# A two-block transformer kernel on one core: other order of the first loads and splits, a norm weight spread by matmul, a last norm by token block, and two adjacent norms computed side by side

## What is computed

```
def rms_norm / rmsnorm(x, g):
    y = x * rsqrt(mean(x * x, axis=-1) + EPS)
    return y * g

def first_block(...):
    for l in range(2):
        x = x + 0.5 * swiglu(rms_norm(x, ffn1_norm[l]), ...)
        ...
        x = x + 0.5 * swiglu(rms_norm(x, ffn2_norm[l]), ...)
    return rms_norm(x, final_norm)

def second_block(...):
    for l in range(2):
        x = x + swiglu_half(rmsnorm(x, g_ffn1[l]), ...)
        ...
        x = x + swiglu_half(rmsnorm(x, g_ffn2[l]), ...)
    return rmsnorm(x, g_final)
```

## Time and profile before

| | us |
|---|---|
| median of 3 runs | 2466.97 (2466.48 to 2468.95) |
| the profiled execution's own time | 2469.05 |
| its span in the profile | 2467.3 |
| PE busy in the span | 2427.1 (98%) |
| DVE busy | 1391.4 (56%) |
| ACT busy | 1175.5 (48%) |
| HBM read | 426.12 MB, 173 GB/s over the span |

### The profile page before, as it was taken

The page is one execution under the profiler, slowest core; times in us unless marked ns, Lnnn a source line. Parts: engine busy times, 40 slices in busy tenths (PEclk is TensorE's granted clock), DMA queues, the critical chain, the costliest instruction groups (busy, mean ns, idle before and its releaser), DMA issues.

```text
span 2467.3 us, 31131 instructions
## 1 busy us (share of the span) xinstructions
PE 2427.1 (98%) x12132; PEld 2038.8 (83%) x12132; DVE 1391.4 (56%) x1297; ACT 1175.5 (48%) x1193; POOL 13.9 (1%) x12
## 2 busy tenths in 40 slices
PE   7999999999999999999999999999999999999998
PEld 6888988788888898888887888878888888887887
DVE  5457855554555577455546546447546456457554
ACT  5445654444444475444445444654445444554443
POOL 0000010000000001000000000000000000000000
PEclk9999999999999999999999999999999999999999
DMA  8554434365565553345555555545655555644653
GB/s 286 187 187 151 157 103 165 109 204 187 178 204 182 170 175 123 121 144 171 184 190 189 187 192 190 159 159 175 196 188 180 191 188 191 189 154 145 205 181 108
DMA packets 329059, 428.41 MB, mean 174 GB/s; under 512 B 15568, under 2 KB 294352, under 8 KB 328720
## 3 DMA queue, kind: packets, MB, share of 16 engines
q1 hardware_dynamic: 325104, 412.48, 51.6%
q10 hardware_dynamic: 3872, 14.75, 1.7%
HBM read 426.12 MB, written 1.05 MB: 173 GB/s over the span
## 4 chain that ended last, share of the span: by engine, by line
PE 93%; ACT 3%; DVE 2%; issue 1%; DMA 1%; ACTq 0%; DVEq 0%; SPq 0%
PE ps L829 28%; PE ps L831 28%; PE ps L830 28%; PE ps L971 2%; PE ps L842 2%; PE ps L1038 1%; ACT whi L451 1%; PE ps L1191 1%; ACT arena L465 1%; PE ps L1091 1%; PE ps L1174 1%; DVE wlo L1342 0%; PE ps L1228 0%; DMA xres<-in_x 0%; PE ps L1093 0%
## 5 line engine op out<-in xcount | busy, mean ns | idle before, releaser
L1342 DVE TENSOR_TENSOR wlo<-raw,whi 128x2048 fp32r<-128x2048 f32 (+1 forms) x395 | 895.5, 2269 | 534.6 <-ACT whi L451 534.4
L451 ACT ACTIVATE whi<-raw 128x2048 fp32r<-128x2048 f32 (+1 forms) x395 | 749.0, 1896 | 442.6 <-PE ps L831 430.4
L829 PE MATMUL ps<-whi,hT_hi 128*128 128x512 f32 x2240 | 890.4, 397 | 7.3 <-DVE hT_lo L1386 2.9
L831 PE MATMUL ps<-whi,hT_lo 128*128 128x512 f32 x2240 | 874.0, 390 | 0.0
L830 PE MATMUL ps<-wlo,hT_hi 128*128 128x512 f32 x2240 | 872.4, 389 | 0.0
L829 PEld LDWEIGHTS ps<-whi,hT_hi 128*128 128x128 f32 x2240 | 424.2, 189 | 92.9 <-issue 4.5
L831 PEld LDWEIGHTS ps<-whi,hT_lo 128*128 128x128 f32 x2240 | 424.0, 189 | 89.2
L830 PEld LDWEIGHTS ps<-wlo,hT_hi 128*128 128x128 f32 x2240 | 424.7, 190 | 82.2 <-issue 0.5
L829 PE MATMUL ps<-whi,aT_hi 128*128 128x512 f32 x640 | 249.9, 390 | 0.0
L831 PE MATMUL ps<-whi,aT_lo 128*128 128x512 f32 x640 | 249.2, 389 | 0.0
L830 PE MATMUL ps<-wlo,aT_hi 128*128 128x512 f32 x640 | 249.1, 389 | 0.0
(11 more groups left out here) (230 smaller groups left out, 1528.3 us busy)
## 6 DMA issues: line engine op xcount, KB each, us to landing
raw<-in_w_ffn SPq DMA_DIRECT2D x264, 512.0 KB, 4.2
raw<-in_w_in SPq DMA_DIRECT2D x144, 512.0 KB, 4.8
raw<-in_ffn_w_down SPq DMA_DIRECT2D x88, 512.0 KB, 4.1
raw<-in_ffn_w_up SPq DMA_DIRECT2D x87, 512.0 KB, 4.0
raw<-in_ffn_w_gate SPq DMA_DIRECT2D x87, 512.0 KB, 4.9
raw<-in_w_out SPq DMA_DIRECT2D x32, 512.0 KB, 4.1
gain<-in_gains ACTq DMA_DIRECT2D x17, 512.0 KB, 4.6
raw<-in_cross_wk SPq DMA_DIRECT2D x16, 512.0 KB, 4.2
```

The costliest lines, as they stand in the source:

```text
L451: act.activation(whi[:, s, :, 0:cols], raw[:, s, :, 0:cols], ACT.Copy).then_inc(hi_ready, 1)
L829: pe.matmul(out, l_hi, r_hi, start=first, stop=False, skip_group_check=True)
L831: return pe.matmul(out, l_lo, r_hi, start=False, stop=last, skip_group_check=True)
L1342: dve.tensor_tensor(wlo[:, s, :, 0:cols], raw[:, s, :, 0:cols], whi[:, s, :, 0:cols].bitcast(F32), ALU.subtract).then_inc(lo_ready, 1)
```

## The change

At the start, only one row of the first gain is loaded (1 x 1024). DVE writes 128 ones into one row of `prod`, and two matmuls of PE multiply the ones by the gain row, which leaves the gain on all partitions in PSUM banks 1 and 3. `first_piece` reads it from there. DVE does pieces 0 and 1, then the first splits, then pieces 2 and 3. ACT rounds unit 2 after the transposes of pieces 2 and 3 instead of before them. The five small loads leave SP's list, and together with table_a and `memx` they are issued by ACT behind the rounding of unit 4.

Between the blocks, `gain_final` puts `xres * final_gain` into a place of its own (`x_gained`) ahead of the split of unit 2, the second norm's sums are taken from `x_gained` without the first norm's factor, and that factor enters as the scale of the second Sqrt.

At the end, the last down unit goes through its pieces as 0, 2, 1, 3. The Sqrt table is loaded by a small activation ahead of the sums. Token block 0 gets its sum and root as soon as its two halves are there, and the second root takes its first half's sum as its bias. ACT issues the last of the four output DMAs.

```diff
@@ sync: ffn, and the output
                 gate_up(off, 0, 0)
-                if b == l == e == 0:
-                    for dst, src in ((lbt[:, :, :], lb), (onorm[:, :, :], out_norm.unsqueeze(0).broadcast_to([P, DEPTH, H_D])),
-                                     (fbias[:, :], f_bias), (wpool[:, :, :, :], w_pool), (pscale[:, :, :], pool_scale)):
-                        sp.dma_start(dst, src).then_inc(loaded, 16)
...
-            for i in range(PIECES):
-                sp.wait_ge(x_ready, PIECES * add_no(1, DEPTH, 0) + i + 1)
+            for n, i in enumerate(LAST_ORDER[:3]):
+                sp.wait_ge(last_out, n + 1)
                 sp.dma_start(piece(o, i), piece(xres, i)).then_inc(stored, 16)
@@ scalar
-            act.dma_start(gain[:, :], gains[0:1, :].broadcast_to([P, DM])).then_inc(gain_loaded, 16)
+            act.dma_start(gain[0:1, :], gains[0:1, :]).then_inc(gain_loaded, 16)
...
+            def joint_squares(n, add):
+                for t in range(TB):
+                    act.wait_ge(x_ready, PIECES * add + 2 + t + 1)
+                    act.activation(sq_junk[:, t * DM:(t + 1) * DM], x_gained[:, t, :], ACT.Square, accum_out=stat[:, 1, 0, t:t + 1]).then_inc(sq_sum, 1)
+                act.wait_ge(sq_sum, 2 * n + 2)
+                act.wait_ge(inv_ready, n)
+                for t in range(TB):
+                    root = act.activation(stat[:, 1, 1, t:t + 1], stat[:, 1, 0, t:t + 1], ACT.Sqrt, scale=stat[:, 1, 2, t:t + 1], bias=EPS)
+                root.then_inc(sq_done, 1)
+
+            def last_norm():
+                act.activation(fin[:, 6:8], ident[:, 0:2], ACT.Sqrt)
+                seen = PIECES * add_no(1, DEPTH, -1)
+                act.wait_ge(x_ready, seen + 2)
+                act.activation(sq_junk[:, 0:DM], xres[:, 0, :], ACT.Square, accum_out=fin[:, 0:1]).then_inc(last_sum, 1)
+                act.wait_ge(last_sum, 1)
+                act.activation(fin[:, 1:2], fin[:, 0:1], ACT.Sqrt, scale=1.0 / DM, bias=EPS).then_inc(last_root, 1)
+                for h in range(2):
+                    act.wait_ge(x_ready, seen + 3 + h)
+                    act.activation(sq_junk[:, DM + 512 * h:DM + 512 * (h + 1)], xres[:, 1, 512 * h:512 * (h + 1)], ACT.Square,
+                                   accum_out=fin[:, 2 + h:3 + h]).then_inc(last_sum, 1)
+                act.wait_ge(last_sum, 3)
+                act.wait_ge(last_bias, 1)
+                act.activation(fin[:, 5:6], fin[:, 3:4], ACT.Sqrt, scale=1.0 / DM, bias=fin[:, 4:5]).then_inc(last_root, 1)
+                act.wait_ge(last_out, PIECES)
+                i = LAST_ORDER[3]
+                act.dma_start(piece(out[0].rearrange("(t p) d -> p t d", p=P), i), piece(xres, i)).then_inc(stored, 16)
...
                     first_split_hi(1)
                     split_hi(b, l, 1)
-                split_hi(b, l, off + 2)
-                turn_out(T, (2, 3))
+                    turn_out(T, (2, 3))
+                    split_hi(b, l, off + 2)
+                else:
+                    split_hi(b, l, off + 2)
+                    turn_out(T, (2, 3))
...
                 if (b, l, e) == (1, 0, 0):
-                    act.wait_ge(inv_ready, n)
-                    squares(xres, n, add + 1, which=1, scale=[stat[:, 0, 2, t:t + 1] for t in range(TB)])
+                    joint_squares(n, add + 1)
@@ tensor
+            pe.wait_ge(first_ones, 1)
+            pe.wait_ge(gain_loaded, 16)
+            for n, bank in enumerate(GAIN_BANKS):
+                pe.matmul(ps[:, bank, :], ones_row, gain[0:1, n * 512:(n + 1) * 512], start=True, stop=True).then_inc(first_gain, 1)
             pe.wait_ge(ident_loaded, 16)
@@ vector
+            def gain_final():
+                for i in range(PIECES):
+                    dve.tensor_tensor(piece(x_gained, i), piece(xres, i), final_gain[:, i // 2 * 512:(i // 2 + 1) * 512], ALU.mult).then_inc(x_ready, 1)
+
             def final_scale(n):
-                inverse(n - 1)
-                for i in range(PIECES):
-                    dve.tensor_tensor(piece(xres, i), piece(xres, i), final_gain[:, i // 2 * 512:(i // 2 + 1) * 512], ALU.mult).then_inc(x_ready, 1)
+                dve.wait_ge(sq_done, n)
+                step(dve.reciprocal(stat[:, 0, 2, :], stat[:, 0, 1, :]))
+                dve.scalar_tensor_tensor(out=stat[:, 1, 2, :], in0=stat[:, 0, 2, :], scalar=1.0 / DM, in1=stat[:, 0, 2, :],
+                                         op0=ALU.mult, op1=ALU.mult).then_inc(inv_ready, 1)
+                for t in range(TB):
+                    scaled = dve.tensor_scalar(xres[:, t, :], x_gained[:, t, :], stat[:, 0, 2, t:t + 1], None, ALU.mult)
+                step(scaled)
                 dve.wait_ge(sq_done, n + 1)
-                for t in range(TB):
-                    last = dve.tensor_scalar(xres[:, t, :], xres[:, t, :], stat[:, 0, 2, t:t + 1], None, ALU.mult)
-                step(last)
...
                 if b == l == e == 0:
                     turn_out(T, (0, 1))
                     first_split_lo(1)
+                    first_piece(2)
+                    first_piece(3)
                     split_lo(b, l, 1)
                 turn_out(T, (2, 3))
+                if (b, l, e) == (1, 0, 0):
+                    gain_final()
                 split_lo(b, l, off + 2)
...
+            def last_output(off):
...
+                def scale(t, root):
+                    dve.wait_ge(last_root, t + 1)
+                    step(dve.reciprocal(fin[:, 8 + t:9 + t], fin[:, root:root + 1]))
+                    for h in range(2):
+                        dve.tensor_scalar(piece(xres, 2 * h + t), piece(xn, 2 * h + t), fin[:, 8 + t:9 + t], None, ALU.mult).then_inc(last_out, 1)
...
+                    if n == PIECES - 1:
+                        dve.wait_ge(last_sum, 2)
+                        dve.tensor_scalar(fin[:, 4:5], fin[:, 2:3], 1.0 / DM, EPS, ALU.mult, ALU.add).then_inc(last_bias, 1)
...
+            dve.memset(ones_row, 1.0).then_inc(first_ones, 1)
+            def first_piece(i):
+                dve.wait_ge(first_gain, i // 2 + 1)
+                dve.wait_ge(x_loaded[i], 16)
+                dve.sem_inc(x_ready, 1)
+                dve.tensor_tensor(piece(xn, i), piece(xres, i), ps[:, GAIN_BANKS[i // 2], :], ALU.mult).then_inc(xn_ready, 1)
+            first_piece(0)
+            first_piece(1)
```

More of the change, by code:

```diff
@@ L37 @@
 S_A, S_B = 3, 2
-V_A, V_B = 30, (12, 10)
+V_A, V_B = 30, (13, 12)
 A_FFN1 = 0
@@ L184, in build @@
         final_gain, joint_gain = zf, hq
+        x_gained = arena[:, 2048 + 6 * 1024:2048 + 8 * 1024].rearrange("p (t d) -> p t d", t=TB)
+        fin = sst[:, 0, :]
+        ones_row = prod[0:1, 0, 0:P]
+        GAIN_BANKS = (1, 3)
+        LAST_ORDER = (0, 2, 1, 3)
         fcs_f, fcs_c, fcs_t = (fcs[0:8, a:a + 256] for a in (0, 256, 768))
@@ L220, in build @@
         first_hi, first_lo = sem("first_hi"), sem("first_lo")
+        first_ones, first_gain = sem("first_ones"), sem("first_gain")
+        last_sum, last_bias, last_root, last_out = (sem(f"last_{n}") for n in ("sum", "bias", "root", "out"))
         tables_loaded = sem("tables_loaded")
@@ L524, in ffn @@
                 split_hi(b, l, off + 4)
+                if b == l == e == 0:
+                    for dst, src in ((lbt[:, :, :], lb), (onorm[:, :, :], out_norm.unsqueeze(0).broadcast_to([P, DEPTH, H_D])),
+                                     (fbias[:, :], f_bias), (wpool[:, :, :, :], w_pool), (pscale[:, :, :], pool_scale)):
+                        act.dma_start(dst, src).then_inc(loaded, 16)
+                    act.dma_start(cst[:, :], table_a).then_inc(tables_loaded, 16)
+                    act.dma_start(memx[:, :, :], mem[0].rearrange("(t p) d -> p t d", p=P)).then_inc(tables_loaded, 16)
                 with act.Fori(0, FF_STEPS - 2) as c:
@@ L818, in _ @@
                 assert count[0] == S_B, ("S_B", count[0])
-            squares(xres, norm_no(1, DEPTH, 0), add_no(1, DEPTH, -1))
+            last_norm()
         @block.tensor
@@ L904, in features_unit, with tall_unit @@
                     then[3]()
-            def tall_unit(b, l, off, lhs, bank, first, last, c=0, T=None, k0=0, signal=None, then={}):
+            def tall_unit(b, l, off, lhs, bank, first, last, c=0, T=None, k0=0, signal=None, then={}, order=range(PIECES)):
                 s = off % RING
                 wait_weights(b, l, off, c)
-                for i in range(PIECES):
-                    half, t = divmod(i, 2)
+                for i, at in enumerate(order):
+                    half, t = divmod(at, 2)
                     if T is not None and half == 0:
@@ L977, in down @@
                     tall_unit(b, l, off, lhs, ACC, first, last, c, signal=acc_done if last else None,
-                              then=then or (turn_ahead(b, T_next) if last else {}))
+                              then=then or (turn_ahead(b, T_next) if last else {}),
+                              order=LAST_ORDER if last and T_next is None else range(PIECES))
```

(3 more changed lines are left out.)

40 lines of the change are left out of this document (25 added, 15 removed).

## The result

The changed kernel takes 2459.04 us in the median of 6 executions (2458.09 to 2460.97), the kernel before 2467.69 of 7: ratio 0.9967, 95% interval 0.9957 to 0.9977. A seventh execution of the changed kernel, at a granted clock of 0.883 instead of 0.995, took 2594.6 and is left out of the median. The profiled execution took 2460.50 (span 2458.6), 8.55 less than the profiled one of before. The forecast was 2457.5, range 2453.5 to 2462.5.

A forecast was written before the change was run, and what follows sets the result against it. PE was taken to bound the kernel (93% of the span). Start -3.0, join -2.25 and -2.5, end -1.7 sum to -9.45 from 2469.05, 2459.6; the median 2.1 lower gives 2457.5 us, range 2453.5 to 2462.5.

The forecast's parts named there:

- Start, -3.0 forecast: At the start: PE's first product 3.5 us earlier, less a 0.5 stall from the swap; bounds -1.5 and -4.
- 512 KB are worth 2.3 us there: Start, ACT's queue: the smaller gain load makes x 2.3 us earlier, and the identity lands at about 7.2.
- I don't expect the first weights to land earlier: Start: the weights come over SP's queue, so ACT rounds the half at 7.81 as now.
- The bound of 12.0: Start: if x gained nothing from the smaller load, PE would start at about 12.0, a gain of 2.3 us.
- The swap, +0.5 forecast: Start, ACT's new order of unit 2's rounding: `prod` comes 1.14 us later, a PE stall of 0.5.
- Was not late: Start: `hT_lo` of piece 2, which the swap serves, was not late in the kernel before.
- Seven loads at nothing: Start: seven load issues on ACT, 3.2 to 5.1 us, are covered up to about 5.9 and cost nothing.
- rival (f): Start: the seven issues on ACT block until their transfers make room, so the kernel is slower, up to 2474; chance 0.05.
- Join, -2.25 and -2.5: Between the blocks: `prod` transposed 2.25 us earlier, waits of 0.6 and 0.7 left, and 2.5 saved as the clock stays up.
- Rival (b): Between the blocks: the clock falls all the same, time 2460.0; chance 0.10.
- End, -1.7: At the end: the last output issue begins at about 2462.45 instead of 2464.15, -1.7 us; bounds -1.2 and -2.1.
- Rival (e): Start: PE's clock is up earlier with the two added matmuls, saving 2.5 us, time 2455; chance 0.08.

The follow-up runs named there:

- s_gainfull: The changed kernel with the first gain loaded to all partitions again (512 KB) and no matmuls spreading it; DVE's new order stays: median 2458.12 us.
- s_loads: The changed kernel with the seven loads put back at their old places on SP and ACT: median 2458.09 us.
- u_join: The changed kernel with the place between the blocks (final gain multiplications and second sums) put back as before: median 2462.21 us.
- u_end: The changed kernel with the last norm put back as before (pieces 0 to 3, both token blocks together, four outputs on SP): median 2461.19 us.
- the repeat: The changed kernel run once more, unedited: median 2458.89 us.
- the faster version: The changed kernel with two gain loads near 1137 earlier, identity load ahead of x, and two gain multiplications and first Squares moved earlier between the blocks: median 2456.41 us.

## Why the prediction was right, and where it was not

- **Start, -3.0 forecast, -2.96 found.** The sum held, its parts did not, and that it held to 0.04 is luck: at the same mark the eight profiles of this start lie 2.8 to 3.9 below the kernel before. The step "512 KB are worth 2.3 us there" held for x but not for the identity, which lands at 8.0 to 8.6, not 7.2; the smaller load brings it 1.0 to 1.6. "I don't expect the first weights to land earlier" was wrong: ACT rounds them at 5.48 instead of 7.81, and s_gainfull (7.97) shows that the gain's size does it, though they come over another queue. So not DVE's split but the transposes bind, and PE begins at 11.20, not 10.85. The bound of 12.0 for no gain from the load was met by s_gainfull, 12.19.
- **The swap, +0.5 forecast.** The stall against the kernel before is 0.31, of which undoing the swap gives back only 0.12. "Was not late" held for `hT_lo` of piece 2 in the old order of DVE; in the new one, without the swap, it is late by 0.2.
- **Seven loads at nothing.** Right (s_loads), and rival (f) is out: 3.8 us of issues, all beside activations. The step to it was wrong on the safe side: ACT begins them 4.7 us before `prod` is transposed, not 1.8, because they do not wait for the activations listed before them.
- **Join, -2.25 and -2.5.** Found 2.24 (15.10 us from piece 3's transposes to those of `prod` before, 12.86 after), and 2.5 for the clock; by u_join the fall costs 1.6 in another execution. The two waits of 0.6 and 0.7 came as 0.55 and 0.51 by the print, 0.7 each in truth. Rival (b) is out: no fall in any profile of the new join, not even behind 2.21 us.
- **End, -1.7.** Found 1.9, by the marks and by u_end.
- **Rival (e)** did not come. The start had 11 slow matmuls, as before; over the profiles it is 6 to 12 with the two added matmuls and 10 to 12 in the three without. Whether they help sometimes, by up to 1 us, stays open. The Trainium skill, "TensorE: Matmul & The Clock Gate", section on the HAM clock gate, says that the number of slow matmuls at a start differs from run to run; these profiles agree, with 6 and 12 on the same code of the start.
- **The median** came out 1.5 above the forecast, and 1.4 above it in the repeat. The three places gave what was forecast, -9.57 by the marks for -9.45. Three things stand between that and the median. The profiled execution had a wait of 1.29 for which the forecast had no term, less 0.33 of drift. The baseline was too low: I put the median 2.1 below the profiled execution, from three runs; seven runs of the kernel before have 2467.69, so 1.36 below, which is 0.7 of the 1.5. And beside the repeat the kernel before had 2466.46, so the change is worth 8.65 by one pair of medians and 7.57 by the other. The places give more than either; what takes the rest back is not shown, since the other executions behind a median have no profile.

## What to carry to other kernels

When one engine is busy for 98% of the span, read its few waits one by one, take each back to the list of the engine that ends it, and put there first what is needed first; three places gave 9.6 us here by the marks, 7.6 and 8.65 by medians, and the faster version found 1.5 more in idle stretches of two other lists. For loads, try it rather than assume it: the identity was needed first, and issuing it first cost 1.1 to 1.7 us. A long wait can cost more behind it through the clock (1.6 and 2.5 us behind 3.6 here), so splitting or shortening one can be worth more than its length. Where executions differ by more than the edits do, compare the times of the same instructions in two profiles, and repeat the profile before believing in a new wait.

## What was not expected of the hardware

- A load's place in the queue can be worth more than its bytes: 64 KB of identity ahead of x made the first piece's multiplication 3.6 us later, and 508 KB more of gain ahead of it 2.2 to 2.7 us. Why, no run shows.
- The same 512 KB load with the same issues around it was used 5.6 to 7.4 us after its issue.
- A smaller load on ACT's queue (4 KB for 512 KB) brought the first weights on SP's queue 2.2 to 2.5 us earlier.
- ACT's DMA issues overlap its activations: all seven (26.40 to 30.23) lay beside two roundings, a table load and two silu, and the first came 3.5 us before the rounding that stands ahead of it in the list.
- A wait of 2.21 us between dense matmuls left the granted clock at 1.00 in the one profile that has it, while waits of 2.2 behind a wait of 1.32 were followed by the lower level 25 times in 28, and waits of 1.31 among small matmuls 9 times in 28.
